# Second-norm rows kept in natural channel order, with every eighth column turned on TensorE

## The reference

```python
    x = x + g1 * (jnp.concatenate([attn, conv_out], axis=-1) @ w_o)
    h2 = _rmsnorm(x, norm2_g) * (1 + sc2) + sh2
    x = x + g2 * _moe(h2, w_router, b_router, w_gate_e, w_up_e, w_down_e,
                      w_gate_s, w_up_s, w_down_s)
...
    scores = jax.nn.sigmoid((xt @ w_router).astype(jnp.float32))
...
    _, eidx = lax.top_k(jnp.where(emask, sel, -jnp.inf), TOP_K)
...
        a = jnp.einsum('nd,edf->nef', xc, w_gate_e)
        b = jnp.einsum('nd,edf->nef', xc, w_up_e)
        hc = jax.nn.silu(a) * b * gc[..., None]
        return jnp.einsum('nef,efd->nd', hc, w_down_e)
...
    shared = (jax.nn.silu(xt @ w_gate_s) * (xt @ w_up_s)) @ w_down_s
```

## Time and profile before

| | us |
|---|---|
| median of 3 runs (1170.70 to 1174.16) | 1171.94 |
| the profiled execution's own time | 1172.41 |
| its span in the trace | 1170.30 |
| PE busy | 1078.9 (92%) |
| DVE busy | 434.1 (37%) |
| second norm and router, about | 435 to 467 |
| expert loop on PE, about | 513 to 1100 |

### The profile page before, as it was taken

How to read it: one execution, slowest core, us unless ns; L and a number is a source line. 1 busy time by engine, 2 the same in 40 slices (tenths; PEclk the granted TensorE clock), 3 DMA queues, 4 the chain that set the end, 5 groups by cost and what they waited for, 6 DMA issues and landing times.

```text
span 1170.3 us, 15543 instructions
## 1 busy us (share of the span) xinstructions
PE 1078.9 (92%) x5582; PEld 523.3 (45%) x5582; DVE 434.1 (37%) x933; ACT 197.9 (17%) x427; POOL 183.6 (16%) x240
## 2 busy tenths in 40 slices
PE   5999899998999996999998889989899798999997
PEld 3355455555777565543343333433334333333332
DVE  0444786404554347731222212222123211223165
ACT  4311111002333014001111111111111111111100
POOL 1012123102120101231111111121111210212100
PEclk9999999996999997999999989999999999999989
DMA  9889799864563932399999999999999999999495
GB/s 314 292 301 319 253 344 318 243 205 179 178 175 108 335 140 95 151 372 384 423 407 417 396 381 410 407 410 401 393 410 405 409 362 421 387 414 379 158 409 214
DMA packets 81055, 372.10 MB, mean 318 GB/s; under 512 B 12513, under 2 KB 27438, under 8 KB 52807
## 3 DMA queue, kind: packets, MB, share of 16 engines
q1 hardware_dynamic: 50160, 269.80, 58.6%
q0 software_dynamic: 23312, 69.67, 17.4%
q10 hardware_dynamic: 7540, 32.07, 7.7%
HBM read 354.24 MB, written 58.01 MB: 352 GB/s over the span
## 4 chain that ended last, share of the span: by engine, by line
PE 75%; DMA 15%; DVE 5%; SPq 2%; issue 2%; ACT 1%; DVEq 0%; POOLq 0%; ACTq 0%
PE pb L1534 23%; PE pb L1552 11%; DMA mem<-in_w_up_e 11%; PE pb L1237 10%; PE pb L1125 5%; PE pb L1392 4%; PE pb L1241 4%; DMA mem<-own_d 2%; PE pb L1152 2%; PE pb L1370 2%; PE pb L1464 2%; PE pb L1311 2%; PE pb L1588 1%; PE pb L1324 1%; DMA mem<-in_w_ada 1%
## 5 line engine op out<-in xcount | busy, mean ns | idle before, releaser
L1534 PE MATMUL pb<-mem 128*32 128x512 f32 (+2 forms) x1600 | 330.7, 618 | 39.4 <-DMA mem<-in_w_up_e 36.5
L1534 PEld LDWEIGHTS pb<-mem 128*32 128x32 f32 (+2 forms) x1600 | 105.4, 134 | 217.0 <-issue 213.2
L1552 PE MATMUL pb<-mem 128*32 128x512 f32 (+2 forms) x800 | 159.9, 596 | 2.7 <-ACT mem L1099 2.7
L2044 DVE SCALAR_TENSOR_TENSOR mem<-pb,mem 128x256 f32<-128x256 f32 x44 | 29.9, 678 | 278.4 <-ACT mem L1095 278.4
L1237 PE MATMUL pb<-mem 128*128 128x384 f32 x384 | 129.1, 490 | 0.0
L1125 PE MATMUL pb<-mem 128*128 128x128 f32 (+3 forms) x593 | 91.6, 287 | 30.4 <-DMA mem<-in_k_cst 11.0
L1125 PEld LDWEIGHTS pb<-mem 128*128 128x128 f32 (+3 forms) x593 | 67.0, 147 | 111.9 <-issue 80.0
L842 POOL DMA_INDIRECT own_d<-mem x44 | 46.4, 1053 | 384.0 <-DVE mem L2051 268.9
L1237 PEld LDWEIGHTS pb<-mem 128*128 128x128 f32 x384 | 71.3, 190 | 57.0 <-issue 9.4
L1552 PEld LDWEIGHTS pb<-mem 128*32 128x32 f32 (+2 forms) x800 | 50.5, 130 | 80.6 <-issue 80.6
L2051 DVE COPY mem<-pb 128x512 f32<-128x512 f32 x44 | 30.4, 691 | 130.2 <-PE pb L1552 130.2
(11 more groups left out here) (264 smaller groups left out, 1008.1 us busy)
## 6 DMA issues: line engine op xcount, KB each, us to landing
mem<-in_w_gate_e SPq DMA_DIRECT2D x64, 1024.0 KB, 11.2
mem<-in_w_up_e SPq DMA_DIRECT2D x64, 1024.0 KB, 15.0
mem<-in_w_down_e SPq DMA_DIRECT2D x64, 1024.0 KB, 13.1
mem<-in_w_ada SPq DMA_DIRECT2D x24, 1024.0 KB, 8.8
mem<-own_d SPq DMA_DIRECT2D x32, 512.0 KB, 12.4
mem<-in_w_in SPq DMA_DIRECT2D x8, 1536.0 KB, 11.7
mem<-new_d POOLq DMA_DIRECT2D x16, 512.0 KB, 7.6
out<-in_cache_k_w ACTq DMA_DIRECT2D x8, 1020.0 KB, 7.3
```

The lines of the kernel that those rows point to most:

```text
L1534: mm = eng.matmul(pb[t % 2][lo:hi, :].rearrange("p (q f) -> p q f", q=2), lhsT=xT[:, k, lo:hi], rhs=wgu[SERVED.index(c) % WB_N][:, :, k, : ...
L1552: mm = eng.matmul(pb[2 + half][lo:hi, :], lhsT=he[:, f, lo:hi], rhs=wdn[SERVED.index(c) % WB_N][:, f, 512 * half:512 * half + 512], start= ...
L2044: eng.scalar_tensor_tensor(out=hh.rearrange("p (k f) -> p f k", k=2), in0=pairs(pb[t % 2][:, FE:2 * FE]), scalar=gd[t][:, 0:1], in1=pairs( ...
```

## The change

`second_norm` reads and writes all three rows without gaps, so that `h2_row`, `h2_d` and the gathered rows `xg` hold the channels in natural order. The rearrangement moves into the turns: turn k takes the columns k, k+8, k+16 and so on, 128 of them, 32 bytes apart. This holds for the five tiles of the shared expert and the router, and for the 45 `x_turn`. Everything that comes out of PSUM is the same as before. Each engine issues the same instructions in the same order as before, with the same waits, the same transfers and the same number of elements; only the access patterns differ.

```diff
-        def chunked(row):
-            return row.rearrange("p (k q) -> p k q", k=KD)
-
-        def strided(row):
-            return row.rearrange("p (q k) -> p k q", k=KD)
+        def every(row, k):
+
+            return row.rearrange("p (q k) -> p k q", k=KD)[:, k, :]
...
-                    mm = turn(pb[2 + k // 4][:, n * (k % 4):n * (k % 4 + 1)], h2_row[j % 2][0:n, P * k:P * (k + 1)], n)
+                    mm = turn(pb[2 + k // 4][:, n * (k % 4):n * (k % 4 + 1)], every(h2_row[j % 2][0:n, :], k), n)
...
-                    mm = turn(pb[4 + k // 4][:, P * (k % 4):P * (k % 4 + 1)], xg[b][:, P * k:P * (k + 1)], P)
+                    mm = turn(pb[4 + k // 4][:, P * (k % 4):P * (k % 4 + 1)], every(xg[b][:, 0:D], k), P)
...
-                row = chunked(h2_row[j % 2][0:n, :])
-                link(eng.scalar_tensor_tensor(out=row, in0=strided(x_t[0:n, tt, :]), scalar=rs2[0:n, tt:tt + 1],
-                                              in1=strided(m2[s][1][0:n, :]), op0=ALU.mult, op1=ALU.mult))
-                eng.tensor_tensor(row, row, strided(m2[s][2][0:n, :]), ALU.add).then_inc(s_h2, 1)
+                row = h2_row[j % 2][0:n, :]
+                link(eng.scalar_tensor_tensor(out=row, in0=x_t[0:n, tt, :], scalar=rs2[0:n, tt:tt + 1],
+                                              in1=m2[s][1][0:n, :], op0=ALU.mult, op1=ALU.mult))
+                eng.tensor_tensor(row, row, m2[s][2][0:n, :], ALU.add).then_inc(s_h2, 1)
```

## The result

The changed kernel takes 1165.1 us (median of 9 runs, 1163.91 to 1169.18) against 1173.2 us for the kernel before (9 runs, 1170.7 to 1176.7). The ratio, estimated from all runs, is 0.9938 (the medians alone would give 0.9931), with a 95% interval from 0.9922 to 0.9953: it is faster by 7.3 us, between 5.5 and 9.2. The forecast was 1187 us. What happened is nearest to the first rival, 1167 us with a step that costs PE nothing: the step did make the loads longer, but hardly any of it reaches the time.

The account below looks back on a forecast made before the run. It took PE to bound the loop's long stretches and expert-weight transfers the short ones. Loop turns +18.1 us, less 1.7 us of clock and 1.9 us of norm, gave +14.5 us on 1172.41: 1187 us, range 1170 to 1202.

Parts of the forecast that it names:

- first rival: Turns on PE: the step costs PE nothing, only DVE's gain of 5.1 us is left, 1167 us; chance 14%.
- price of a turn: PE's weight load of a stepped turn: 1.87 ns a column, 240 ns for 128 columns, too long to hide.
- upper bound: Eight turns on PE: at most 1.2 us more, with 251 ns a load and 10 ns between loads.
- 190 by adding: Rival for a turn's load: step added to its own fast load, 190 ns instead of 240, 1171 us; chance 10%.
- comparison with the streaming: Turns on PE: a load hides behind about 0.11 us of streaming 128 columns; at 240 ns it can't.
- 1.05 us for eight turns: Turns on PE: added cost of eight stepped turns, 8 x (0.24 - 0.11).
- account of the loop: Expert loop: 39 `x_turn` cost 41.0 us, less 22.9 us given back by waits and slow clock, +18.1 us.
- B: PE's wait at a round's last tile, t10: 4.57, 4.00, 6.15 and 1.78 us; expected gone or nearly so.
- DVE part: Second norm before the loop: two instructions at 1219 ns each, 1.67 us saved a tile, 8.3 us for five.
- -1.9 us in the sum: Norm and router stage: the part of DVE's gain left if eight turns take 2.0 us; bounds 0 and -8.3.
- sign that I named: Loop loads of L1125: 0.33 us if the forecast holds; 141 ns means a wrong load price, near 1167 us.

Follow-up runs that it names:

- E6: Changed kernel with the loop's turns as ordinary float32 matmuls against the identity, loading every eighth column; ratio 1.0833 to the kernel before.
- E5: Kernel before with the loop's turns as ordinary float32 matmuls against the identity, on adjacent columns; ratio 1.0157 to the kernel before.
- E1: Changed kernel with the loop's turns taking 128 adjacent columns again; ratio 0.9926 to the kernel before.
- E9: The changed kernel run once more, unaltered, beside others on the same chip; ratio 0.9945 to the kernel before.
- E2: Kernel before with only the loop's turns taking every eighth column; ratio 0.9992 to the kernel before.
- E7: Kernel before with the loop's turns taking every second column, 8 bytes apart; one execution, 1178.9 us.
- E8: Kernel before with the loop's turns taking every fourth column, 16 bytes apart; one execution, 1171.5 us.
- E4: Changed kernel with a third h2_row buffer, DVE set-up moved behind the norms, and ACT copying the sample tile before its last squares; ratio 0.9931 to the kernel before.
- E11: Kernel before with the loop's turns taking every fourth column, as a timed run; ratio 1.0016 to the kernel before.

## Why the prediction was wrong

- **The step that failed** is the price of a turn: "Then 128 columns take 128 x 1.87 = 240 ns". The load took 193 ns, or 106 without the fixed part. The error was to carry a rate from the load of a matmul to the load of a turn. The rows had warned: 190 and 141 ns for the same 128 columns say that a turn's load runs at 0.42 ns a column where a matmul's takes 0.80. I saw this, named it under the first rival, and gave it 14%; what stood against it were the 147 - 113 = 34 ns between the two forms of 32 columns. The 10 ns between loads in the upper bound were my estimate, and no row or run shows them. Neither reading that I priced (240, and 190 by adding) was the true one. The factor of the rows, 1.87 / 0.80 = 2.3, on the turn's own 54 ns would have given 126 ns; measured are 106 with this step, and 209 - 87 = 122 with the 16-byte step from which the factor comes.
- **The comparison with the streaming** was right: what matters is 0.11 us. The load came out at 0.11, not 0.24, so the 1.05 us for eight turns were 0.01 to 0.07. E6 shows the other side of it, where the load is longer: 247 ns, and 0.25 us a pass.
- **The account of the loop** then had nothing to act on. Tested with real work in E5 it was 5 us short of 18. It didn't ask what is late next once B is gone; three new waits of 9.3 us in all are what E5's trace shows, and what they wait for is argued only.
- **The DVE part** was right: 1284 and 1225 ns for the 1219 that I took, and for cheap turns "some 5.1 us earlier", measured 5.3. It left out that the clock can take a part of it back or add to it. That the first rival's 1167 us came so close is in part luck: its 5.1 us are right for the stage, 2.2 us of them are left at the second tile in the traces of the two kernels, and the runs gained 7.3. The -1.9 us in the sum hung on dear turns and fell with them.
- **The sign that I named** was a bad one: "0.33 us or 141 ns" left out everything between, and 193 ns at hardly any cost was what came. The sign to name was the pace of the turns with few columns to stream.
- The traced 5.3 us lie just beside the interval of 5.5 to 9.2 us. E1 gives 8.7 (6.2 to 11.1) and E9 6.5 (4.1 to 8.9) us. Whether the rest is more than scatter stays open. No stage of the traces shows a second gain of its own, but the place of the lower clock moves single traces by up to 5 us, as shown above; a share of the 7.3 us may come from there.

## What to carry to other kernels

A gap in an access pattern had a price here on both engines that read it, and it was worth moving to where that price lies behind something as long: DVE paid 1.6 us for each tile in full, PE's loads pay about 50 ns each and hide nearly all of it. Before using a rate from one kind of weight load for another, compare the two kinds without the gap; if they differ, scale by the factor (here 2.0 on a turn's load and 2.4 on a matmul's for the same 32 bytes), and keep the absolute rate as the other bound. And when added work is to vanish in a wait, look at the next transfer in the queue as well: the wait that vanishes may have covered it. A gain of a few us before a loop should be read from several traces, since the lower clock moves too.

## What was unexpected of the hardware

- The load of a float32 turn takes 141 ns for 128 columns (loop, kernel before and E1), that of a float32 matmul 190 to 192 ns (L1534 before, L1518 in E5). With a step of 32 bytes they take 193 ns (changed kernel, E2) and 334 ns (E6).
- For a turn's load, steps of 8 and 16 bytes cost more (209 ns in E7 and E8) than 32 bytes (193 ns), and none of the three leaves the load at its 141 ns. Why the wider step is cheaper isn't settled.
- Taking one wait of PE away moved the idle time by a few us, and the stretch at the lower clock with it (E4). PE was done with the first prompt tile's turns 440.68 - 433.05 = 7.6 us after the first norm instruction, instead of 443.59 - 429.60 = 14.0, and the stage was no shorter.
- The same norm and router take 31.8 us in one trace and 35.2 in another (before, E11), and the first 16 matmuls of the loop 7.1, 8.8 or 9.8 us (before, E1, changed kernel), by where the lower clock falls.
